# Four of eight memory-attention units set between the differential heads' blocks, and no barrier ahead of the last projection

## The reference

```python
y_mla = mla_branch(...)    # 8 heads of causal attention, head width 96, values 64
y_diff = diff_branch(...)  # 4 heads, each with two causal maps: (p0 - lam * p1) @ v,
                           # then an RMS norm over the head's 64 values
y_mem = mem_branch(...)    # 4 heads that attend to 256 memory tokens, no mask
y = jnp.concatenate([y_mla, y_diff, y_mem], axis=-1) * jax.nn.silu(z)
x = x + y @ w_out
```

## Time and profile before

| what | value |
|---|---|
| median of 3 runs | 3324.51 us (3322.49 to 3331.71) |
| the profiled execution's own time | 3326.73 us |
| its span, first to last instruction | 3325.0 us, mean granted clock 0.980 |
| busy: PE, PEld | 3141.4 us (94%), 2454.1 us (74%) |
| busy: DVE, ACT, POOL | 1818.5 us (55%), 984.0 us (30%), 930.7 us (28%) |
| DMA | 196.42 MB, mean 59 GB/s |

### The profile page before, as it was taken

The page is one execution under the profiler, slowest core; times in us unless marked ns, Lnnn a source line. Parts: engine busy times, 40 slices in busy tenths (PEclk is TensorE's granted clock), DMA queues, the critical chain, the costliest instruction groups (busy, mean ns, idle before and its releaser), DMA issues.

```text
span 3325.0 us, 37517 instructions
## 1 busy us (share of the span) xinstructions
PE 3141.4 (94%) x14298; PEld 2454.1 (74%) x14298; DVE 1818.5 (55%) x3020; ACT 984.0 (30%) x1899; POOL 930.7 (28%) x613
## 2 busy tenths in 40 slices
PE   7899999888889999989999999999989999898799
PEld 3678888665668878878888788888868887565567
DVE  1369999478854457760332544344234616856761
ACT  3230111477751015560102100001213211656650
POOL 0223323000003226653333332333322443401112
PEclk9999999999999999999999999999999999999889
DMA  8121332100001111123343111112111211000002
GB/s 207 47 65 48 95 100 94 76 20 20 20 26 51 51 32 39 39 58 105 98 139 98 36 51 51 45 51 101 64 58 60 75 51 35 1 1 7 1 33 113
DMA packets 189465, 196.42 MB, mean 59 GB/s; under 512 B 12657, under 2 KB 152429, under 8 KB 188525
## 3 DMA queue, kind: packets, MB, share of 16 engines
q1 hardware_dynamic: 173117, 137.89, 14.5%
q10 hardware_dynamic: 16176, 56.18, 4.5%
HBM read 153.15 MB, written 40.89 MB: 58 GB/s over the span
## 4 chain that ended last, share of the span: by engine, by line
PE 76%; DVE 8%; ACT 5%; issue 5%; POOL 2%; DVEq 1%; POOLq 1%; ACTq 1%; DMA 1%; SPq 0%
PE psum L686 72%; PE psum L690 4%; ACT arena L1527 2%; DVE rounded L2019 2%; DVE arena L2185 2%; POOL rounded L1352 1%; DVE arena L2019 1%; DVE arena L2662 1%; POOL stat L1341 1%; ACT arena L1681 1%; ACT arena L1987 1%; DVE arena L2022 1%; DVE arena L2173 1%; POOLq L1351 1%; ACT rounded L1641 0%
## 5 line engine op out<-in xcount | busy, mean ns | idle before, releaser
L686 PE MATMUL psum<-rounded,rounded 128*128 128x512 f32 (+2 forms) x9664 | 2257.2, 392 | 52.1 <-DVE rounded L2019 23.4
L686 PEld LDWEIGHTS psum<-rounded,rounded 128*128 128x128 f32 x9664 | 1816.4, 189 | 452.4 <-issue 57.8
L686 PE MATMUL psum<-arena 128*128 128x512 f32 (+11 forms) x2514 | 702.0, 435 | 35.2 <-ACT arena L1527 20.9
L1350 POOL CAST rounded<-arena 128x1024 fp32r<-128x1024 f32 (+1 forms) x190 | 207.2, 1091 | 1565.0 <-DMA arena<-in_w_in 783.4
L686 PEld LDWEIGHTS psum<-arena 128*128 128x128 f32 (+3 forms) x2514 | 381.6, 192 | 238.0 <-issue 183.2
L1527 ACT ACTIVATE arena<-psum 128x512 f32<-128x512 f32 (+9 forms) x572 | 309.3, 569 | 808.9 <-PE psum L686 653.8
L1352 POOL TENSOR_TENSOR rounded<-arena,rounded 128x1024 fp32r<-128x1024 f32 (+1 forms) x190 | 467.7, 2462 | 28.2 <-issue 1.3
L690 PE MATMUL psum<-ident,arena 128*128 128x128 f32 (+1 forms) x1784 | 268.2, 290 | 80.6 <-ACT arena L1527 24.9
L690 PEld LDWEIGHTS psum<-ident,arena 128*128 128x128 f32 (+1 forms) x1784 | 221.6, 148 | 146.9 <-issue 53.9
L2019 DVE TENSOR_TENSOR rounded<-arena,rounded 128x1024 fp32r<-128x1024 f32 (+3 forms) x164 | 214.0, 1336 | 212.2 <-ACT rounded L1530 157.4
L2019 DVE TENSOR_TENSOR arena<-arena,psum 128x512 f32<-128x512 f32 (+1 forms) x144 | 105.5, 745 | 361.6 <-PE psum L686 333.9
(11 more groups left out here) (167 smaller groups left out, 1543.9 us busy)
## 6 DMA issues: line engine op xcount, KB each, us to landing
arena<-in_w_in SPq DMA_DIRECT2D x84, 512.0 KB, 3.7
arena<-in_w_ffn_up SPq DMA_DIRECT2D x44, 512.0 KB, 3.8
arena<-in_w_ffn_down SPq DMA_DIRECT2D x22, 512.0 KB, 3.6
gate_d<-arena ACTq DMA_DIRECT2D x16, 512.0 KB, 3.8
z_d<-arena ACTq DMA_DIRECT2D x32, 256.0 KB, 3.0
arena<-in_w_ssm_out SPq DMA_DIRECT2D x16, 512.0 KB, 4.2
arena<-z_d SPq DMA_DIRECT2D x32, 256.0 KB, 3.1
arena<-gate_d ACTq DMA_DIRECT2D x16, 512.0 KB, 3.5
```

Of the source, the lines that this page charges most:

```text
L686: return pe.matmul(out, lhsT, rhs, start=start, stop=stop)
L1350: pool.tensor_copy(high_part, raw)
```

## The change

It places four memory units (heads 0 and 1, both halves) after blocks 5 of differential head 0, 1 and 5 of head 1, and 1 of head 2, so that four stay at the end. Because heads no longer have 16 units each, their starts are kept in `diff_start`. `y2_at` counts from the list's end and takes in part 6, the parts have the order `Y2_ORDER`, and the loops have four more steps in relation to the list's length. `end_phase` ahead of the projection goes on four engines. The remaining weights of the projection are gated by the last memory sweep in place of phase 10, and ScalarE's load of `xo` follows part 7 directly.

```diff
@@ -283,7 +283,7 @@
             w_wide(("z", c), w_in, 8, O_Z + 512 * c, 512, split=True)
         for n in range(GATES_EARLY, 2 * KT):
             gate_weight(n)
-        PH_MERGE, PH_OUT2 = 4, 10
+        PH_MERGE = 4
         XBC_ORDER = [*range(16, XT), *range(16)]
         next_slot[0] = 0
         for j in range(XT):
@@ -316,7 +316,7 @@
         for c in range(2):
             for k in range(0, 8, 2):
                 first = c == 0 and k < 6
-                gate = (("PV", "m", MLAH - 1, 1) if k == 0 else ("PV", "d", DH // 2 - 1, 1)) if first else PH_OUT2
+                gate = (("PV", "m", MLAH - 1, 1) if k == 0 else ("PV", "d", DH // 2 - 1, 1)) if first else ("PV", "e", MEMH - 1, 1)
                 weight((("o2", c), k), [(2, 512, 0, 512, w_o2[:, k:k + 2, 512 * c:512 * c + 512])], gate, True,
                        k if first else None)
 
@@ -545,10 +545,11 @@
         squared_n = {name: n + 1 for n, name in enumerate(sq_order)}
 
 
+        Y2_ORDER = (0, 1, 2, 3, 4, 6, 5, 7)
         part_order = [(key, k) for key, n in (("hA", KT), ("hB", KT), ("y", 2 * KT), ("att", KT), ("m", KT), ("h2", 2 * KT))
                       for k in range(n)]
         part_order += [("act", c, k) for c in range(2) for k in range(FT)]
-        part_order += [(key, k) for key, n in (("h3", 2 * KT), ("y2", KT)) for k in range(n)]
+        part_order += [("h3", k) for k in range(2 * KT)] + [("y2", k) for k in Y2_ORDER]
 
         def high(name):
 
@@ -601,7 +602,17 @@
                     "m", i, i + 1, qTm[0:MQK, h, i * P:(i + 1) * P],
                     lambda lo, hi, h=h: kTm[0:MQK, h, lo:hi],
                     lambda b, h=h: vM[:, b, (h // 2) * P:(h // 2 + 1) * P], h=h, mask=strip[:, (7 - i) * P:S]))
+        def memory_unit(h, half):
+
+            r, j, i = 64 * (h % 2), h // 2, 4 * half + 3
+            return unit("e", i, 2 * 4, [pB[r:r + 64, i - 3 + n, 768 + j * P:768 + (j + 1) * P] for n in range(4)],
+                        kmT[r:r + 64, j, :],
+                        lambda b, h=h: memkv[:, b, 256 + (h // 2) * P:256 + (h // 2 + 1) * P], h=h, four=(2 * h + half) % 3)
+
+        between = {(0, 5): (0, 0), (1, 1): (0, 1), (1, 5): (1, 0), (2, 1): (1, 1)}
+        diff_start = []
         for h in range(DH // 2):
+            diff_start.append(len(subs2))
             for i in range(TT):
                 for m in (2 * h, 2 * h + 1):
                     subs2.append(unit(
@@ -609,13 +620,11 @@
                         lambda lo, hi, h=h, m=m: maps[h % 2][2 + m % 2][:, lo:hi],
                         lambda b, h=h: pB[:, b, 512 + (h // 2) * P:512 + (h // 2 + 1) * P], h=h, m=m,
                         mask=strip[:, (7 - i) * P:S]))
-        for h in range(MEMH):
-            for i in (3, 7):
-                r, j = 64 * (h % 2), h // 2
-                subs2.append(unit(
-                    "e", i, 2 * 4, [pB[r:r + 64, i - 3 + n, 768 + j * P:768 + (j + 1) * P] for n in range(4)],
-                    kmT[r:r + 64, j, :],
-                    lambda b, h=h: memkv[:, b, 256 + (h // 2) * P:256 + (h // 2 + 1) * P], h=h, four=len(subs2) % 3))
+                if (h, i) in between:
+                    subs2.append(memory_unit(*between[h, i]))
+        for h in range(2, MEMH):
+            for half in range(2):
+                subs2.append(memory_unit(h, half))
 
         def first_map(u):
 
@@ -656,13 +665,13 @@
 
         turned_at = {n + T_LAG: n for n in blocks2}
         summed_at = {n + PV_LAG: n for n in sweeps2}
-        STEPS2 = len(subs2) + PV_LAG + 2
-        halved_at = {N_MLA + 16 * (h - 1) + 2 * p: (h, p) for h in range(DH // 2) for p in range(4)}
-        mapped_at = {N_MLA + 16 * (h - 1) + 4 + n: (h, n) for h in range(DH // 2) for n in range(8)}
+        STEPS2 = len(subs2) + PV_LAG + 6
+        halved_at = {diff_start[h] - 16 + 2 * p: (h, p) for h in range(DH // 2) for p in range(4)}
+        mapped_at = {diff_start[h] - 12 + n: (h, n) for h in range(DH // 2) for n in range(8)}
         pair_end = {j: max(n for n in sweeps2 if subs2[n]["ph"] == "d" and subs2[n]["h"] == 2 * j + 1) + PV_LAG + 1
                     for j in range(2)}
 
-        y2_at = {N_MLA + 65 + 2 * k: k for k in range(5)}
+        y2_at = {len(subs2) - 7 + 2 * n: Y2_ORDER[n] for n in range(6)}
 
         def last_group(u):
             return (u["nk"] - 1) // 4
@@ -1194,9 +1203,9 @@
             pe.wait_ge(phase_done, 4 * 9)
 
             for s in range(STEPS2):
-                if s - N_MLA in range(0, 16 * (DH // 2), 16):
+                if s in diff_start:
                     for n in range(8):
-                        pe.wait_ge(*written(("map", (s - N_MLA) // 16, n)))
+                        pe.wait_ge(*written(("map", diff_start.index(s), n)))
                 if s < len(subs2):
                     u, name = subs2[s], ("S", N1 + s)
                     out = bank(name, 1 if u["nk"] <= 4 else 2)
@@ -1247,7 +1256,6 @@
                         pe.wait_ge(sub_spread, j + 1)
                         for half in range(2):
                             four(("sr", j, half), [rs_wide[:, 4 * half + n, :] for n in range(4)])
-            end_phase(pe)
             for c in range(2):
                 token_rows_parts(("o2", c), 512, 8, y2hi, y2lo, "y2" if c == 0 else None)
 
@@ -1514,8 +1522,6 @@
             power(("sub", 0))
             split_weights(*[(("o2", 0), k) for k in (2, 4)])
             power(("sub", 1))
-            end_phase(pool)
-            pool.wait_ge(phase_done, 4 * 10)
             split_weights((("o2", 0), 6))
             split_weights(*[(("o2", 1), k) for k in range(0, 8, 2)])
 
@@ -2001,16 +2007,15 @@
                     k = y2_at[s]
                     if k < 4:
                         act.wait_ge(*written(("PV", "m", MLAH - 1, 1)))
+                    elif k == 4:
+                        act.wait_ge(sub_gated, 1)
                     else:
-                        act.wait_ge(sub_gated, 1)
+                        act.wait_ge(*written(("PV", "e", 1, 1)))
                     high_part(y2hi[k], zT[:, k, :])
             act.wait_ge(sub_gated, 2)
             high_part(y2hi[5], zT[:, 5, :])
-            for k in (6, 7):
-                act.wait_ge(*written(("PV", "e", 2 * (k - 6) + 1, 1)))
-                high_part(y2hi[k], zT[:, k, :])
-            end_phase(act)
-            act.wait_ge(phase_done, 4 * 10)
+            act.wait_ge(*written(("PV", "e", MEMH - 1, 1)))
+            high_part(y2hi[7], zT[:, 7, :])
             act.dma_start(xo.rearrange("p a n -> p (a n)"), x3_d).then_inc(back_in[3], 16)
 
         @block.vector
@@ -2628,7 +2633,7 @@
                         dve.drain()
                         dve.tensor_scalar(p, p, r, None, ALU.mult).then_inc(probs_ready, 1)
                     else:
-                        p0, sum0 = probs2[probs_slot(n - 1)][:, 0:w], rsum[:, n % 8 - 1:n % 8]
+                        p0, sum0 = probs2[probs_slot(n - 1)][:, 0:w], rsum[:, (n - 1) % 8:(n - 1) % 8 + 1]
                         c = 2 * u["i"] + u["h"] % 2
                         dve.reciprocal(r, rsum[:, n % 8:n % 8 + 1])
                         dve.tensor_scalar(sub_eps[u["h"] // 2][:, c:c + 1], sum0, sum0, EPS, ALU.mult, ALU.mult)
@@ -2692,9 +2697,8 @@
                 if s - 1 in y2_at:
                     k = y2_at[s - 1]
                     low_part(("y2", k), y2lo[k], zT[:, k, :], y2hi[k])
-            for k in (5, 6, 7):
+            for k in (5, 7):
                 low_part(("y2", k), y2lo[k], zT[:, k, :], y2hi[k])
-            end_phase(dve)
             dve.wait_ge(back_in[3], 16)
             for c in range(2):
                 for tt in range(TT):
```

## The result

The changed kernel takes 3353.89 us in the median (3344.28 to 3358.87), the kernel before 3326.69 in the same comparison (3322.49 to 3331.71): 1.0081 times as long, with a 95% interval of 1.0069 to 1.0094. Forecast were 3322.5 us, with a range that ended at 3332. So it is 27 us slower, where I had no change. The five executions of the changed kernel lie up to 14.6 us apart, and their granted clock goes with their time: 0.977 in the fastest, 0.972 to 0.973 in the other four. The one that was traced is the slowest, 3358.87 us; against the traced execution of the kernel before it took 32.1 us more, not 27. Stages are read from single executions throughout, so a difference of up to about 2 us in one head may be scatter.

The account below looks back on a forecast made before the run. TensorE's idle time and clock were taken to bound the kernel. Tail -11.5, slower projection start +1.8 and moved units +7.7 gave -2.0 us on 3326.73, thus 3324.7; that execution lay 2.2 over the median, so 3322.5 us, range 3308 to 3332.

Parts of the forecast that it names:

- 11.5 us of gain in the tail: Tail: with four units fewer, the projection starts 17.8 us after the last differential sweep, 11.5 us earlier relative to preceding units.
- 7.7 of cost in the heads: Differential heads: the four moved units cost 6.0 + 7.0 us, less 5.3 of clock given back, +7.7 us.
- the very chain named: Tail after the sweep: GpSimd's two splits, then its power, VectorE's spread, TensorE's transposes and hand-overs, 17.8 us to the projection.
- the row parts moved into head 3: Parts 0 and 1, made in blocks 6 and 7 of head 3 on a busy VectorE, 1.23 us each: +2.4 us.
- The barrier: Ahead of the projection: TensorE never waited for it and the weights are covered before and after, so removal brings 0 us.
- the two units after block 5: Heads 0 and 1: VectorE's 2.45 us on the path, TensorE's transposes and sweep 0.5; 3.0 us each, 6.0 for both.
- the two after block 1: Heads 1 and 2: scores 1.99 us on the path, VectorE's work free in its wait, 1.5 for the rest; 3.5 us each.
- the upper bound: Differential heads: +19.6 us for four units if each takes its full TensorE time, 4.9 us, and no clock comes back.
- a clock held up by more work: Starts of heads 1 and 2: TensorE works through them, so 10.6 us at half clock go, 5.3 us gained.
- The slower rival: Heads pay in full, 4.9 us a unit; banks held through four exponentials add two 1.96 us waits; 3338.3 us, chance 0.13.
- friction: Heads 0 to 2: 19.6 us of TensorE work fits into 21.7 us of idle time, but not without friction.

Follow-up runs that it names:

- e1: The changed kernel with all eight memory units back at the end of the list, the rest of the change kept: 3326.52 us.
- e2: The changed kernel with the phase barrier ahead of the projection put back on four engines and the weights gated by it: 3355.02 us.
- e3: The changed kernel with only head 0's two units moved (after block 5 of head 0 and block 1 of head 1), six at the end: 3336.44 us.
- e5: The changed kernel with two needless 512-column matmuls ahead of the scores of each differential unit of blocks 4 to 7, 64 in all: 3339.33 us.
- e6: The same 64 needless matmuls in the kernel with all eight memory units at the end (e1): 3329.94 us.
- e11: The changed kernel without the preparation of differential head 2's queries and keys during head 1: 3340.61 us.
- e12: The kernel with all eight units at the end (e1), without the preparation of differential head 2's queries and keys: 3323.58 us.
- e9: The changed kernel with VectorE copying memory scores out of PSUM first, to free their banks early, plus the 64 matmuls of e5: 3350.16 us.
- e8: The changed kernel with only head 0's two units moved, after blocks 1 and 5 of the last differential head, six at the end: 3324.37 us.
- e10: The changed kernel with only the two units after block 5 of heads 0 and 1 moved, six at the end: 3334.72 us.

## Why the prediction was wrong

**The frame held, the price of a moved unit didn't.** I set 11.5 us of gain in the tail against 7.7 of cost in the heads. The tail's part was right: 12.9 us from the last mask on. The sweep took 7.55 us (8.10 forecast), the projection began 17.3 us after it (17.8), by the very chain named, and its 384 matmuls took 88.89 us, 1.6 more (1.8). Of the row parts moved into head 3, charged at 2.4, about 2.1 show, between the first two reductions of the tail. The barrier was worth 0, as e1 and e2 show.

**The failed step is "the two units after block 5" and "the two after block 1".** I put the first at 3.0 us each: 2.45 of VectorE on the path, everything else in gaps. One cost 7.4 us in its own head and 1.7 in the next. The assumption that failed is that TensorE's work in the gaps of about 1 us was free. Over heads 0 to 2 its busy time grew by 34.8 us, more than the 19.6 of four units at full clock, and its idle time by 5.5: the work was added in full, much of it at half clock, and the gaps stayed. In head 0's timeline they end with ScalarE's copies. That added work moves such gaps along the chain in place of filling them is my reading; shown is that they stayed. The others, 3.5 us, I put where VectorE waits for a sweep; in e3 one costs 9.1. TensorE's idle time in heads 0 to 2 went from 21.7 to 27.2 us, where I had it filled. At nearly full clock a unit costs 6.9 us (e5 against e6), above even the 4.9 that I had taken as the upper bound. And I gave no price to the next head's preparation, which rides on the same steps: e11 and e12 put it, for one head, at 9 to 10 us of the loss.

**The clock went the other way.** I gave back 5.3 us for a clock held up by more work. Low time rose from 17.5 to 54 us, and e5 shows that at least 12.1 us hang on it, since that gain is net of the matmuls added. The sign was the error: more work in the heads did not hold the clock up, and much of the work there ran at 1.2 GHz.

**The slower rival came nearest, and was too small.** It named the held banks and a price of 4.9 us a unit plus 1.96 for two, and gave 3338.3. Its place was right (TensorE does wait for ScalarE, 1.78 us behind head 0's unit), and its 23.5 us for four units stand against 40.3 measured. Its mechanism is the smaller part: with the clock up, an early release of the banks gains nothing (e9 against e5). The range left it out at 0.13; what I had called friction was the larger number. The passage of the Trainium skill that speaks of oscillation by short idles ("TensorE: Matmul & The Clock Gate", "A second HAM failure mode: psum-queue depth-cycling") spoke against this change, and I had drawn only a gain from the page. The trace agrees with it in the heads that took units (0.87, 0.79, 0.77), and not in e6's head 0, which idles 3.7 us in short gaps at 1.00.

**What stays open.** Which part of a unit brings the clock down isn't told: its waits, or its matmuls on 64 rows and its transposes. How far the missing preparation explains the cheap last head isn't either. What the tail gives back depends on which units leave it: 10.3 us for head 0's two (56.3 to 46.0, in e8 and in e3), but only 5.1 for the first halves of heads 0 and 1 (51.2, in e10), which I didn't follow up; 2.2 more for all four (46.0 to 43.8). With six units left there, their sweeps cover the norm's chain; with four it ends last, so the second pair was also more than the tail can repay.

## What to carry to other kernels

Idle time spread over a loop in which each engine waits for the next isn't room for more work: price an inserted unit at no less than its whole work on the engine that waits, here 4.9 us, where 6.9 to 10.1 were paid in heads 0 to 2, and ask for evidence, such as a place where such a unit already stands, before calling any of it hidden. Look at what else rides on the same steps. Taking work off a tail pays only until the next chain there shows; price the first and the last unit taken away apart. Where the granted clock changes within the stage, take it from a run as a cost or a gain of its own; here its sign was the opposite of the one that more work suggested.

## What the runs showed of the hardware

Useless work made a kernel faster: 64 matmuls of 512 columns, overwritten at once, took 14.6 us off the change, with TensorE's clock up from 0.77 to 0.87 to 0.95 to 1.00 in three heads. The granted clock also stayed at 1.2 GHz under a TensorE that the trace shows busy without a pause. In the tail of the kernel before, slices of 4 us:

```profile
3186.00:3190.00 4.00, 4.00 (x11) 2.66 (x9) 3.29 (x4) 3.82 (x13) 0.00 (x0) 0.50 0.00 0
3190.00:3194.00 4.00, 4.00 (x14) 3.10 (x14) 3.76 (x6) 3.77 (x16) 0.00 (x0) 0.50 0.00 0
3194.00:3198.00 4.00, 4.00 (x14) 3.07 (x13) 2.09 (x2) 1.73 (x5) 0.00 (x0) 0.50 0.02 4
3198.00:3202.00 4.00, 4.00 (x10) 1.71 (x9) 1.58 (x3) 0.00 (x0) 0.00 (x0) 0.97 0.00 0
```

In the first three TensorE runs memory scores, on 64 rows, and transposes; the clock rises once the sweep of 128 rows by 512 columns has begun. And in the changed kernel's head 0 it fell without a long wait ahead of it:

```profile
3062.00:3066.00 4.00, 2.38 (x16) 1.84 (x16) 3.57 (x12) 3.45 (x9) 3.39 (x4) 1.00 0.10 36
3066.00:3070.00 4.00, 3.28 (x14) 2.45 (x14) 2.65 (x4) 2.96 (x7) 1.16 (x1) 0.87 0.01 2
3070.00:3074.00 4.00, 3.09 (x12) 2.10 (x10) 3.37 (x6) 2.68 (x10) 0.00 (x0) 0.50 0.00 0
```

From 3060 to 3070 the longest gap of TensorE is 1.19 us. A head's clock can't be told from its idle time alone.
